# The second block's mixer with both scan directions side by side, pipelined attention and 64-column states, in a two-block fp32 kernel on one core

## What is computed

```
h = rms_norm(x); proj = h @ w_in[l]            # 1792 columns rwkv, 1536 attention, 2048 gates
o_a = rwkv7_mixer(p_rwkv)                      # per head and direction, state S of 64 x 64:
    sa = -S kk_t;  S = S*w_t + sa (kk_t*a_t)' + v_t k_t';  y_t = S r_t      # 8 heads
    y = scan forwards + scan backwards, group norm, + bonus * v, * gate
o_b = diff_attention(p_attn)                   # 4 heads of 128, two score maps each, softmax with ALiBi
merged = sum over the 2 branches of sigmoid(gates) * (branch @ w_branch)
x = x + merged @ w_out
```

## Time and profile before

| | us |
|---|---|
| median of 3 runs | 3593.78 (3591.69 to 3596.24) |
| profiled execution | 3603.26, span 3601.5 |
| PE busy in the span | 3208.2 (89%), granted clock 0.926 |
| DVE busy | 1527.6 (42%) |
| ACT busy, POOL busy | 802.5 (22%), 656.5 (18%) |
| first rw product to first branch product, layer 0 and 1 | 354.6 and 355.1 |

### The profile page before, as it was taken

The page is one execution under the profiler, slowest core; times in us unless marked ns, Lnnn a source line. Parts: engine busy times, 40 slices in busy tenths (PEclk is TensorE's granted clock), DMA queues, the critical chain, the costliest instruction groups (busy, mean ns, idle before and its releaser), DMA issues. The chain is left out here.

```text
span 3601.5 us, 50884 instructions
## 1 busy us (share of the span) xinstructions
PE 3208.2 (89%) x21719; PEld 2186.4 (61%) x21719; DVE 1527.6 (42%) x2513; ACT 802.5 (22%) x1096; POOL 656.5 (18%) x596
## 2 busy tenths in 40 slices
PE   7987999999598889999949997888998998688899
PEld 3765343443266534434319985776798987677698
DVE  1324332332453432323356465443555555644354
ACT  1211111111022111111114343120333334221232
POOL 3511233333262123333320000110000000101000
PEclk9978999999797899999979997888999999798899
DMA  8635999999872599999975431003555533011362
GB/s 281 229 139 225 396 384 387 389 381 373 308 251 111 216 410 382 382 379 387 386 285 202 157 109 68 25 26 114 181 185 170 188 116 112 25 48 61 116 211 82
DMA packets 305356, 799.20 MB, mean 222 GB/s; under 512 B 57030, under 2 KB 155868, under 8 KB 251244
## 3 DMA queue, kind: packets, MB, share of 16 engines
q1 hardware_dynamic: 245804, 727.16, 53.4%
q0 software_dynamic: 58784, 66.69, 5.6%
q10 hardware_dynamic: 544, 2.10, 0.1%
HBM read 988.65 MB, written 53.48 MB: 289 GB/s over the span
## 5 line engine op out<-in xcount | busy, mean ns | idle before, releaser
L811 PE MATMUL f_bank<-f_ringA,f_arena 128*64 128x512 f32 x3072 | 687.8, 601 | 14.6 <-DMA f_ringA<-in_w_up,f_chosen 13.5
L811 PEld LDWEIGHTS f_bank<-f_ringA,f_arena 128*64 128x64 f32 x3072 | 216.2, 138 | 405.9 <-issue 404.7
L2112 PE MATMUL s_bank<-s_hT_high_parts,s_ringA_parts 128*128 128x256 f32 x1344 | 380.4, 283 | 0.0
L2112 PE MATMUL s_bank<-s_hT_parts,s_highA_parts 128*128 128x256 f32 x1344 | 380.3, 283 | 0.0
L2112 PE MATMUL s_bank<-s_hT_high_parts,s_highA_parts 128*128 128x256 f32 x1344 | 380.2, 283 | 0.0
L832 PE MATMUL f_bank<-f_ringB,f_arena 128*64 128x512 f32 x1536 | 346.1, 592 | 2.1 <-DVE f_arena L1598 2.1
L1583 DVE TENSOR_TENSOR f_arena<-f_arena,f_bank 128x256 f32<-128x256 f32 x96 | 58.8, 613 | 594.7 <-ACT f_arena L1193 594.7
L1114 ACT ACTIVATE f_arena<-f_bank 128x512 f32<-128x512 f32 (+1 forms) x266 | 144.8, 583 | 609.3 <-PE f_bank L792 373.3
L2112 PEld LDWEIGHTS s_bank<-s_hT_high_parts,s_highA_parts 128*128 128x128 f32 x1344 | 257.9, 192 | 1.4
L2112 PEld LDWEIGHTS s_bank<-s_hT_parts,s_highA_parts 128*128 128x128 f32 x1344 | 257.9, 192 | 1.4
L2112 PEld LDWEIGHTS s_bank<-s_hT_high_parts,s_ringA_parts 128*128 128x128 f32 x1344 | 257.9, 192 | 0.0
(11 more groups left out here) (422 smaller groups left out, 5350.0 us busy)
## 6 DMA issues: line engine op xcount, KB each, us to landing
f_ringA<-in_w_gate SPq DMA_DIRECT2D x128, 1024.0 KB, 8.9
f_ringA<-in_w_up SPq DMA_DIRECT2D x128, 1024.0 KB, 11.5
f_ringB<-in_w_down SPq DMA_DIRECT2D x128, 1024.0 KB, 12.2
s_ringA<-in_ffn_in SPq DMA_DIRECT2D x88, 1024.0 KB, 7.7
f_ringA<-in_w_ada SPq DMA_DIRECT2D x46, 1024.0 KB, 8.3
s_arena<-in_ffn_out SPq DMA_DIRECT2D x44, 1024.0 KB, 6.4
s_ringA<-in_w_in SPq DMA_DIRECT2D x40, 1024.0 KB, 7.1
f_ringA<-in_w_in SPq DMA_DIRECT2D x28, 1024.0 KB, 10.0
```

The lines of the kernel that those rows point to most:

```text
L811: last = mm(ps[j * CAP:(j + 1) * CAP, :].rearrange("p (h c) -> p h c", h=2), picked[:, b % 2, k, j * CAP:(j + 1) * CAP], gu[j][:, :, k, :] ...
L2112: last = mm(ps[:, t * S:(t + 1) * S], parts_of(wx[:, k, cs_]), parts_of(hx[:, k, :]), start=(k == 0 and x == 0), stop=(k == DT - 1 and x = ...
```

## The change

Everything lies in the mixer of `second_block`.

- `w_in`'s chunks come in another order: low-rank inputs first, then k, r, v. Between their groups PE makes decay and rate of both directions and the sums of k*k; the norm of k is a reciprocal of 8 rows of 256, spread to the heads by a matmul (L2303).
- Attention is pipelined: ten half gates lie between scores, turns and values. DVE does both directions' running sums, keys and scalings between the attention's operations. The factor 1+(iclr-1)*k_a goes to ACT. The 16 scans of 64 columns become 4 scans of 256, with zeros in `starts` at the chunk's starts.
- Grams, masks and inversion run over four units, both directions side by side. A mask of 512 columns replaces two of 256. DVE makes the level masks; GpSimd makes none.
- The state has 64 columns for each head: no off-diagonal blocks, no mask by heads. State products are 16 matmuls of 64x64 a direction and chunk (before 8, each with 128x128 outputs), SA 8 (4 before). Both directions' Y add up in the same banks YA and YB. The scans alternate chunk by chunk; four half gates lie in them and two behind them.
- ACT copies YA, DVE adds YB. The load of `w_out` waits for YA.

The core of the diff:

```diff
         MIX = 7
+        rw_tiles = [(12, 13), (14,), (4, 5), (6, 7), (0, 1), (2, 3), (8, 9), (10, 11)]
...
-                chunks += list(zip(edges, edges[1:]))
+                chunks += [(1536, CRW), (512, 1024), (0, 512), (1024, 1536)]
...
-                for d in range(2):
-                    for lv in range(LEVELS):
-                        for q in range(2):
-                            if lv == 0:
-                                pool.wait_ge(u_ready, 2 * d + q + 1)
-                            if lv >= 2:
-                                banks.read(pool, ("W", d, q, lv - 2))
-                            nc.gpsimd.tensor_tensor(Z[lv % 2][:, q], U[:, q], spread(masks[:, 7 + lv, :], 1, 8),
-                                                    ALU.mult).then_inc(z_ready, 1)
...
+                half_gates(0)
+                score(3)
+                half_gates(1)
+                score(4)
+                half_gates(2)
+                turn_comb(0)
+                score(5)
+                half_gates(3)
+                values(0)
+                score(6)
+                half_gates(4)
+                turn_comb(1)
+                score(7)
+                half_gates(5)
+                values(1)
+                half_gates(6)
+                turn_comb(2)
+                half_gates(7)
+                values(2)
+                half_gates(8)
+                turn_comb(3)
+                half_gates(9)
+                values(3)
...
+                gram(0, 0)
+                gram(0, 1)
+                tokens_first(1)
+                gram(1, 0)
+                pe.wait_ge(ob_ready, 1)
+                to_features(("obT",), ob, 2)
+                gram(1, 1)
...
+                    for i in range(4):
+                        d, q = i // 2, i % 2
+                        pe.wait_ge(z_ready, 4 * lv + i + 1)
+                        if lv:
+                            banks.evacuated(pe, ("dX", i, lv - 1))
+                        else:
+                            pe.wait_ge(start_ready, i + 1)
+                        ps = banks.claim(pe, ("W", i, lv))
+                        banks.fill(own_blocks(ps, Z[d][:, q], X[d][:, q]), ("W", i, lv))
+                    for i in range(4):
+                        d, q = i // 2, i % 2
+                        banks.evacuated(pe, ("W", i, lv))
+                        if lv < LEVELS - 1:
+                            ps = banks.claim(pe, ("dX", i, lv))
+                            banks.fill(own_blocks(ps, XT[d][:, q], W1[d][:, q]), ("dX", i, lv))
+                        ps = banks.claim(pe, ("dXT", i, lv))
+                        banks.fill(own_blocks(ps, W1[d][:, q], XT[d][:, q]), ("dXT", i, lv))
...
+                    if n < NCH - 1:
+                        ps = [banks.claim(pe, ("state", d, n)) for d in range(2)]
+                        for d in range(2):
+                            c = scan_order[d][n]
+                            o, m = (c % 2) * CH, c // 2
+                            for p, hh, cs_ in heads():
+                                mm(ps[d][hh * HD:(hh + 1) * HD, p * HD:(p + 1) * HD], Ktok[d][o:o + CH, m, cs_],
+                                   Vtok[o:o + CH, m, cs_], start=(p == 0), stop=False, skip_group_check=True)
+                        for d in range(2):
+                            c = scan_order[d][n]
+                            o, m = (c % 2) * CH, c // 2
+                            if n:
+                                pe.wait_ge(sa_ready, 2 * (n - 1) + d + 1)
+                            src = SA[d] if n else SA0[d]
+                            for p, hh, cs_ in heads():
+                                last = mm(ps[d][hh * HD:(hh + 1) * HD, p * HD:(p + 1) * HD], Btok[d][o:o + CH, m, cs_],
+                                          src[o:o + CH, m, cs_], start=False, stop=True, skip_group_check=True)
+                            banks.fill(last, ("state", d, n))
+                    if n < 2:
+                        from_keys(n)
...
+                    half_gates(2 * GATES_EARLY + n)
+                pe.wait_ge(sa_ready, 2 * (NCH - 1))
+                for d in range(2):
+                    last = from_steps(d, NCH - 1)
+                    banks.fill(last, ("YA", scan_order[d][NCH - 1] // 2))
+                half_gates(14)
+                half_gates(15)
                 for m in range(MT):
...
+                running(0)
+                biased(0)
+                biased(1)
+                running(1)
+                biased(2)
+                biased(3)
+                for g in range(2):
+                    key = ("kkb", g)
+                    ps = banks.read(dve, key)
+                    banks.free(tt(kk[:, 2 * g:2 * g + 2, :], kk[:, 2 * g:2 * g + 2, :], pair_of(ps), ALU.mult), key)
+                for g in range(2):
+                    banks.evacuated(dve, ("kkb", g))
+                keys(0)
+                combine(0)
+                biased(4)
+                biased(5)
+                scaled(0)
+                combine(1)
+                biased(6)
+                biased(7)
+                keys(1)
+                combine(2)
+                scaled(1)
...
+                def masked(d, q):
+                    for hh in range(2):
+                        us = slice(4 * hh, 4 * hh + 4)
+                        for name, out in (("UR", UM[d]), ("KR", KM[d])):
+                            key = (name, d, q, hh)
+                            ps = banks.read(dve, key)[:, :].rearrange("p (n r t) -> p n r t", n=4, r=2)
+                            banks.free(tt(out[:, q, us], ps, spread(masks[:, d:d + 3:2, :], 1, 4), ALU.mult), key)
+                        key = ("L", d, q, hh)
+                        ps = banks.read(dve, key)[:, 0:S].rearrange("p (n t) -> p n t", n=4)
+                        banks.free(tt(X[d][:, q, us, :], ps, mask(4 + d, 4), ALU.mult), key)
+                    banks.evacuated(dve, ("L", d, q, 1))
+                    step(tt(XT[d][:, q], UM[d][:, q, :, 0, :], mask(6, 8), ALU.mult))
+                    tt(X[d][:, q], X[d][:, q], mask(12, 8), ALU.add)
+                    tt(XT[d][:, q], XT[d][:, q], mask(12, 8), ALU.add).then_inc(start_ready, 1)
+                def level_mask(i, lv):
...
+                def level_mask(i, lv):
+                    d, q = i // 2, i % 2
+                    tt(Z[d][:, q], UM[d][:, q, :, 0, :], mask(7 + lv, 8), ALU.mult).then_inc(z_ready, 1)
+                banks.evacuated(dve, "bonus")
+                masked(0, 0)
+                masked(0, 1)
+                level_mask(0, 0)
+                level_mask(1, 0)
...
+                    if lv < LEVELS - 1:
+                        for i in range(4):
+                            banks.read(dve, ("W", i, lv))
+                            level_mask(i, lv + 1)
+                    for i in range(4):
```

More of the change, by code:

```diff
@@ new lines, in plan @@
+            for m in range(MT):
+                banks.take(("o", m), m)
+            for s in range(2 * BH):
+                banks.take(("score", s), 2 + s % 3)
+            for h in range(BH):
+                banks.take(("combT", h), 5)
+            for g in range(GATES_EARLY):
+                banks.take(("gates", g), 6 + g % 2)
+            for m in range(MT):
+                banks.take(("Btok", 0, m), 2 + m)
+                banks.take(("Ktok", 0, m), 4 + m)
+            turn = itertools.cycle((7, 2, 3, 4, 5, 0, 1, 6))
@@ L1849, in plan @@
                 for q in range(2):
[L1850 to L1852 removed]
+                    banks.take(("SA0", 2 * d + q), 1 + 4 * q)
                     for half in range(2):
[L1854 to L1859 removed]
@@ L1860, in plan @@
-                for g in GATES_BESIDE[d]:
-                    banks.take(("gates", g), 4 + g % 2)
-                for m in range(MT):
-                    banks.take(("Y", d, m), 2 + m)
-            for m in range(MT):
-                banks.take(("gate", m), 6 + m)
+                        banks.take(("XAT", 2 * d + q, half), (((0, 3), (2, 7)), ((4, 3), (6, 7)))[d][q][half])
+            for n in range(NCH):
+                if n:
+                    for hh in range(2):
+                        banks.take(("SA", n, hh), hh)
+                if n < NCH - 1:
+                    for d in range(2):
+                        banks.take(("state", d, n), 4 + d)
@@ L1866, in plan @@
+            for m in range(MT):
+                banks.take(("YA", m), 2 + m)
+            banks.take("YB", 6)
+            for g in range(GATES_EARLY, 8):
+                banks.take(("gates", g), 7)
+            for m in range(MT):
+                banks.take(("gate", m), 4 + m)
             for g in range(2):
-                banks.take(("oaT", g), 4 + g)
+                banks.take(("oaT", g), g)
             for t in range(DT):
-                banks.take(("branch", t), t % 4)
+                banks.take(("branch", t), (2, 3, 6, 7)[t % 4])
@@ L2268, in tensor @@
+                score(2)
+                pe.wait_ge(mixed_ready, 8)
```

(30 more changed lines are left out.)

953 lines of the change are left out of this document (473 added, 480 removed).

## The result

The changed kernel takes 3449.28 us (median; 3446.67 to 3455.0), the kernel before in the same session 3595.01 (3591.69 to 3596.28): 145.7 us less, ratio 0.9598 (95% interval 0.9582 to 0.9615). The forecast was 3465, 130 less. The two profiled executions lie 154.3 apart (span 3601.5 and 3447.2), because the one of before was 8 us above its median and the one after at it.

What follows compares the result with a forecast made beforehand. PE was taken to wait for DVE in attention, masks and tail and to limit inversion and scan. Terms -32, -3, -2, -32.6, +1.5 make -68, with handoffs -65 a layer, -130 in all: 3465 us, range 3430 to 3525.

Steps and rivals of the forecast that it cites:

- Step 1, attention: From the first rwkv product to the last attention values: 151.5 us becomes 119.5, -32 a layer.
- Step 2, masks: From the last values to masks ready: 35.7 us where it was 38.9, -3 a layer.
- Inversion: 54 blocks of 16 matmuls at 0.93 us plus 1.8 at half clock: 52 us, limited by PE.
- the first rival: VectorE becomes the limit of the inversion: +13 us a layer, 3491; chance 0.07.
- SA0 and XAT: Work behind the inversion's levels: 16.2 us for both directions plus 1.3 for ACT's copies, 17.5.
- Scan: Four half gates at 14.4 us and 320 small matmuls at 0.09, 28.8: 43.2 us, -32.6 a layer.
- The second rival: Small matmuls don't pair, 0.136 to 0.27 us each: scan 15 to 58 us longer a layer, 3495 to 3580; chance 0.08.
- The 3.5 us for handoffs: Allowance for handoffs of scan steps left out of the sum: -68 becomes -65 us a layer.
- Tail: Behind the scan, with a copy and additions ahead of the group norm: 19.1 us for 17.6, +1.5.
- The signs that I had named: Trace windows expected after the change: mixer 280 to 300 us, scan 40 to 50, tail 18 to 20, attention clock above 0.85.
- Attention without overlap: Rival: late combines make PE stand before each turn in attention: +30 us a layer, 3525; chance 0.07.
- The clock: Slower case: TensorE at its low clock in inversion, SA0, XAT and scan: +45 us a layer, about 3685; chance 0.05.

Runs made afterwards that it cites:

- e4: Changed kernel with four of the attention's ten half gates put behind its last values; 3472.35 us, ratio 0.9656 to the kernel before.
- e7: Changed kernel with e1's alternating steps products and three of the scan's four half gates moved to where TensorE waits; 3421.16 us, ratio 0.9505.
- e1: Changed kernel with the scan's steps products into Y issued alternately for the two directions, not in blocks of eight; 3442.61 us, ratio 0.9567.
- e8: Changed kernel with rwkv columns in the old order (low-rank inputs last) and both directions' decay and rate behind them all; 3445.03 us, ratio 0.9589.
- e9: e7 with the decay and rate products behind all rwkv groups, the low-rank columns still first; 3404.11 us, ratio 0.9468.
- e2: Changed kernel with the scan's head order turned round, so consecutive state products lie in the same half of the array; 3451.22 us, ratio 0.9593.
- e3: Changed kernel with all 20 level masks of a layer on GpSimd again; 3450.61 us, ratio 0.9586.

## Why the prediction was right, and where it was off

The forecast came out 16 us above the measured time, and its mechanism holds. Inside it two terms were wrong by more than 5 us each, the low-rank products and the small matmuls of the scan, and part of the agreement is luck, as told at each step.

**Bound.** PE waited for DVE in attention, masks and tail, and was the limit in inversion and scan: right. e4 and e7 show it from both sides. Four half gates taken out of the attention cost 13 of their 14.6 us; three taken out of the scan give back 11.1 beside e1's 3.2.

**Step 1, attention: -32, measured -30.2 (151.5 to 121.3) and -33.0 in layer 1 (152.4 to 119.4).** This total is right by errors that cancel. PE is through with the rwkv columns at 61.2 us and not 55.5, as the starts in the changed kernel's timeline and the window below show:

```profile
2154.01 2.87 PE L2237 MATMUL s_bank<-s_arena,s_w 64*128 64x256 f32 x8 [1.46 <-ACT s_arena L2590]
2156.66 3.62 PE L2237 MATMUL s_bank<-s_arena,s_a 64*128 64x256 f32 x8
2168.30 1.99 PE L2237 MATMUL s_bank<-s_arena,s_w 64*128 64x256 f32 x8
2170.14 1.89 PE L2237 MATMUL s_bank<-s_arena,s_a 64*128 64x256 f32 x8
2185.66 1.14 PE L2270 MATMUL s_bank<-s_arena 64*128 64x256 f32 x8
```

```profile
2156.00:2164.00 8.00, 8.00 (x28) 6.60 (x27) 3.93 (x5) 3.67 (x10) 0.00 (x0) 0.50 0.00 0
```

The 3.7 us for decay and rate of both directions is what one direction's take; these are the kernel before's, in its timeline:

```profile
2231.13 1.99 PE L2281 MATMUL s_bank<-s_arena,s_w 64*128 64x256 f32 x8
2232.97 1.89 PE L2281 MATMUL s_bank<-s_arena,s_a 64*128 64x256 f32 x8
```

A product of decay or rate is four matmuls, a score only two. Both directions need some 7.4 by that price, and took some 10, since the first ran while the granted clock was 0.50 (1.2 GHz) from 2156 to 2164, after PE had waited 1.5 us for ACT; the rwkv products behind it lost some time to that too. The small sums of k*k took 1.9, less than the forecast left for them.

Behind PE, DVE was as forecast: 5.2 us to the first running sum (5.0 forecast; the norm's reciprocal 1.74 for 1.6), and 48.6 for its chain (48.0; a running sum's scans 2.36 where I chose 2.4 between 0.76 and 3.0). So the running sum starts at 66.4 and not 60.5, and the last combine is ready at 115.0 instead of 109.5. PE gets to it only at 116.5.

On PE's side the recorded terms behind 55.5 add up to 117.6; the 119.5 has 1.9 us that no term explains. PE took 60.1 us for that stretch where the terms have 62.1, as the first combine cost 0.5 of waiting and not 4. e8 and e9 show what the late last group is worth: with the low-rank products behind it, DVE starts 10.9 us earlier.

**Step 2, masks: 35.7 forecast, 34.5.** The 5.7 a unit and the 0.69 for a level mask came out. **Inversion: 52 forecast (of which 51.3 behind the masks), 52.1** (0.966 a block with its slow start). DVE had 35.6 us to do in 52, so the first rival, VectorE as the limit, is out. **SA0 and XAT: 17.5 forecast, 13.9.** This term was mis-sized by 3.6. It was twice the window of one direction, each with a wait of 1.59 us ahead of the states, and 1.3 for ACT's copies; with four units in one run a single wait of 1.15 is left, and the 1.3 didn't come.

**Scan: 43.2 forecast, 36.7.** The largest error. The half gates took 14.6 (14.4 forecast), so the term that was mis-sized is the price of a small matmul: 0.09 taken, 0.069 measured on average, inside the lower bound's 0.058 to 0.083. Even that average hides 0.05 for SA and 0.114 for the last steps products, so that it lay in the bound is in part luck. The second rival (no pairing, 0.136 and more) is out: the dearest that was read in any scan is 0.114. The 3.5 us for handoffs came from the 3.6 of waits before; the two directions cover each other, and 0.6 is left. **Tail: 19.1 forecast, 20.2.**

Together 278.6 where 289.5 was forecast (286 + 3.5): SA0 and scan with handoffs 13.6 better and masks 1.2, attention, inversion and tail 3.7 worse.

**The signs that I had named.** The mixer's window came out below the 280 to 300 that I gave (278.6 and 275.4), the scan below its 40 to 50, and 16 small matmuls at 0.75 to 1.82 and not 1.1 to 1.7. DVE was busy for 41.0 of the 50 us ahead of the last values, where I had 45 or more, since it was through with its chain 6 us earlier. The tail was 0.2 over its 18 to 20. The last values (121.3) and the clock in the attention (0.92) were as said.

**The rivals.** Attention without overlap: out by the 0.5 us of waits at L2280. The clock: 0.91 to 1.00 in every stage that PE bounds, in spite of the 8 us at 0.50, so the slower case had no footing. The scan's windows go from 0.87 to 1.00 as its waits go. By the Trainium skill, TensorE: Matmul & The Clock Gate, Part 1, the slow state is the default and activity lifts it; the scan's rows agree.

## What to carry to other kernels

Where two engines take turns, list each wait of the limiting one and each piece of its work that no one is waiting for, and put the second into the first; a piece that lies in a stage where the engine is full is the one to move. Price small matmuls by the nearest block of the same shape and order in the trace, and look at which rows and output rows follow each other: swapping two loops cost nothing here. When a stage that ran once for each direction is put in one place, count its matmuls again for both. Ahead of moving work earlier on one engine, see what it pushes back on the next engine's in-order queue.

## What the runs showed that was not expected

- The order of 64x64 matmuls alone sets their price: 16 steps products 1.82 us in blocks of one direction, 1.08 alternating (e1); 16 state products some 0.75 alternating, some 1.2 in blocks (e2). Which of rows, output rows and bank does it was not taken apart, nor why the steps products are the dearer ones in either order.
- The granted clock differs between layers with the same instructions: 0.91 and 0.98 in e9's first stage and attention, 8.3 us of difference. With the same code up to there, that stage ended at 117.3 us in e1 and at 121.5 in the changed kernel, so single windows of this stage tell nothing below some 4 to 8 us. The scan's, with the clock at 1.00, agree to 0.1 between the layers (36.7 twice, e1 33.5 and 33.4).
- GpSimd slows not one but all three of a unit's masks from SBUF, which the prediction had only for L2933 (1.16): their means were 0.95, 1.16 and 1.16 us before and 0.956, 0.930 and 0.951 in e3, with single ones up to 1.75. In the changed kernel they are at 0.69.
